# Lists of a mixture-of-experts kernel copied from a DRAM table instead of computed by matmuls, and a new order of row sums at its end

## The reference, cut to what matters

```
scores = sigmoid(t @ router_w)                    # 384 tokens x 64 experts
... group-limited choice: 8 experts for each token
w = take(scores, idx); w = w / sum(w) * 2.5       # gates of the chosen ones
hid = silu(t @ w_gate[e]) * (t @ w_up[e]) * gate  # FF = 256, per expert
routed = sum over e of hid @ w_down[e]
x = x + gate2 * (routed + shared expert)
y = rmsnorm(x, final_g)
```

## Time and profile before

| | us |
|---|---|
| median of 3 runs (lowest to highest) | 1182.12 (1181.52 to 1184.41) |
| the profiled execution | 1182.67 |
| its span, first to last instruction | 1180.8 |
| before the expert loop | 0 to about 516 |
| expert loop | about 516 to 1141 |
| end | about 1141 to 1180.8 |
| mean granted TensorE clock | 0.987 of full |

### The profile page before, as it was taken

One profiled execution on the slowest core, in us unless ns is written; L12 is line 12 of the kernel. 1 busy time (PEld: TensorE's weight loads), 2 busy tenths in 40 slices (PEclk: granted clock), 3 DMA queues, 4 the chain that ended last, 5 costly groups with the idle time before them and its releaser, 6 DMA issues.

```text
span 1180.8 us, 16797 instructions
## 1 busy us (share of the span) xinstructions
PE 1130.6 (96%) x5641; PEld 921.2 (78%) x5641; DVE 1029.9 (87%) x1378; ACT 801.3 (68%) x996; POOL 241.5 (20%) x184
## 2 busy tenths in 40 slices
PE   4999999998999999989999999999999999999995
PEld 1699999864557798658888888888888888888862
DVE  4769999989996565769999999999999999999976
ACT  6543232777873642648888888888888888888832
POOL 1000000001113001212523223333233323232210
PEclk9999999998999989999999999999999999999998
DMA  9673446635447227858999999999999999999994
GB/s 347 187 183 107 141 150 169 180 119 173 160 131 227 76 92 260 324 227 319 382 370 373 368 381 367 378 362 354 348 352 356 367 357 376 363 378 361 355 415 176
DMA packets 123036, 328.06 MB, mean 278 GB/s; under 512 B 28281, under 2 KB 69848, under 8 KB 98152
## 3 DMA queue, kind: packets, MB, share of 16 engines
q1 hardware_dynamic: 98368, 289.34, 66.7%
q0 software_dynamic: 21648, 33.80, 8.5%
q10 hardware_dynamic: 2968, 4.26, 1.0%
HBM read 326.66 MB, written 41.66 MB: 312 GB/s over the span
## 4 chain that ended last, share of the span: by engine, by line
PE 86%; DVE 5%; ACT 4%; DMA 3%; issue 1%; SPq 0%; POOLq 0%; ACTq 0%; DVEq 0%
PE bank L1755 22%; PE bank L1757 22%; PE bank L1756 22%; PE bank L1765 8%; PE bank L1950 2%; ACT hi L819 2%; PE bank L1938 2%; PE bank L2081 1%; DMA raw<-in_mod_w_dram 1%; DVE lo L1194 1%; PE bank L1771 1%; PE bank L1772 1%; PE bank L2200 1%; DMA xg<-h_d,ixt 1%; PE bank L2230 1%
## 5 line engine op out<-in xcount | busy, mean ns | idle before, releaser
L1463 DVE TENSOR_TENSOR lgu<-raw,hgu 128x2048 fp32r<-128x2048 f32 x128 | 292.1, 2282 | 2.3 <-ACT hgu L1072 2.3
L1072 ACT ACTIVATE hgu<-raw 128x2048 fp32r<-128x2048 f32 x128 | 245.2, 1916 | 0.0
L1755 PE MATMUL bank<-hgu,xgh 128*128 128x512 f32 x512 | 206.6, 404 | 0.4 <-issue 0.3
L1757 PE MATMUL bank<-hgu,xgl 128*128 128x512 f32 x512 | 201.4, 393 | 0.0
L1756 PE MATMUL bank<-lgu,xgh 128*128 128x512 f32 x512 | 199.7, 390 | 0.0
L1592 DVE TENSOR_TENSOR lo<-raw,hi 128x2048 fp32r<-128x2048 f32 x64 | 147.6, 2306 | 25.7 <-ACT hi L1081 21.5
L1194 DVE TENSOR_TENSOR lo<-raw,hi 128x2048 fp32r<-128x2048 f32 (+2 forms) x57 | 125.6, 2207 | 29.6 <-ACT hi L819 29.6
L777 POOL DMA_INDIRECT xg<-h_d,ixt x64 | 66.3, 1036 | 391.2 <-DVE gsl L1565 367.6
L786 POOL DMA_INDIRECT y_d<-ys,ixt x62 | 130.2, 2100 | 48.3 <-ACT ys L1114 28.6
L1292 DVE SCALAR_TENSOR_TENSOR zb<-zb,cwt 128x400 f32<-128x400 f32 x240 | 135.6, 630 | 0.6
L1081 ACT ACTIVATE hi<-raw 128x2048 fp32r<-128x2048 f32 x64 | 122.9, 1921 | 14.6 <-DMA raw<-in_exp_w_down_dram 14.4
(11 more groups left out here) (312 smaller groups left out, 2085.7 us busy)
## 6 DMA issues: line engine op xcount, KB each, us to landing
raw<-in_exp_w_gate_dram SPq DMA_DIRECT2D x64, 1024.0 KB
raw<-in_exp_w_up_dram SPq DMA_DIRECT2D x64, 1024.0 KB
raw<-in_exp_w_down_dram SPq DMA_DIRECT2D x64, 1024.0 KB
raw<-in_mod_w_dram SPq DMA_DIRECT2D x20, 1024.0 KB, 5.2
raw<-in_w_in_dram SPq DMA_DIRECT2D x16, 512.0 KB, 5.3
raw<-in_w_in_dram SPq DMA_DIRECT2D x8, 1024.0 KB, 5.3
mraw<-in_mod_w_dram SPq DMA_DIRECT2D x4, 1024.0 KB, 15.7
raw<-in_w_o_attn_dram SPq DMA_DIRECT2D x4, 1024.0 KB, 5.0
```

The source lines that it names most:

```text
L1072: act.activation(hgu[k % 2][:, :, w, :], src, ACT.Copy).then_inc(ghi_done, 1)
L1463: dve.tensor_tensor(lgu[k % 2][:, :, w, :], src, hgu[k % 2][:, :, w, :].bitcast(F32), ALU.subtract).then_inc(glo_done, 1)
L1755: pe.matmul(out, ah, bh, start=first, stop=False)
L1757: return pe.matmul(out, al, bh, start=False, stop=last)
```

## The change

1. Lists. Only the first 19 experts (`ON_TENSOR`) get their list by `onehot` and `token_list`. For these and the later ones, 24 small DMAs write a table `lists_d` in DRAM: one 16-byte entry (token row, destination row, gate) for each token and choice. `entry_rows` prepares the entries' rows on VectorE ahead of the loop, `entry_gates` their gates, two in each of steps 2 to 13, and `write_lists` issues two writes of 128 entries on GpSimd's queue in the same steps, behind that step's gather and scatter. In step 14 the table is read back to SBUF (`listed`). For experts from 19 on, `list_of` is two copies from `listed`.
2. The table is filled with ones near the start of the kernel by a DMA from GpSimd's queue.
3. A second block of 8 steps is written out ahead of the device loop (`BLOCKS`).
4. The load of `fgr` moves from ahead of the loop to the step with `left == 3`, the 62nd.
5. End: tile 0 takes residual and gate after row 5, then rows 6 and 7 scaled one by one; TensorE adds row 7 of tile 1 ahead of row 6 of tile 2.
6. Two pairs of semaphores are merged; two constants are added (88 columns).

```diff
+            pool.wait_ge(con_in, 16)
+            pool.dma_start(lists_d.rearrange(...), ones.unsqueeze(1).to_broadcast([P, NJ * 4 // P, P])).then_inc(lists_out, 16)
...
+            def write_lists(first):
+                for n in (first, first + 1):
+                    t, u = n // TOPK, n % TOPK
+                    pool.wait_ge(entry_done, n + 1)
+                    pool.indirect_dma_start(lists_d, bass.IndirectOffsetOnAxis(ap=entry_row[:, t, u:u + 1], axis=0),
+                                            entry[:, t, u, :], None,
+                                            bounds_check=P * NJ - 1, oob_is_err=False).then_inc(lists_out, 16)
...
+                if isinstance(j, int) and FIRST_SENT <= j < FIRST_SENT + 12:
+                    write_lists(2 * (j - FIRST_SENT))
+                if isinstance(j, int) and j == FIRST_SENT + 12:
+                    pool.wait_ge(lists_out, 16 * (NT * TOPK + 1))
+                    pool.dma_start(listed[:, :, :], lists_d.rearrange("(q j) v -> q j v", q=P)).then_inc(lists_out, 16)
...
+                if left == 3:
+                    listed_all = value(act, i * UNROLL + UNROLL)
+                    act.wait_ge(rtab_done, 1)
+                    act.wait_ge(list_done, listed_all)
+                    act.dma_start(fgr[:, :], final_g...partition_broadcast(P)).then_inc(tail_in, 16)
...
-            act.wait_ge(x1_out, 48)
-            act.dma_start(fgr[:, :], final_g...partition_broadcast(P)).then_inc(tail_in, 16)
...
+                if not isinstance(j, int) or j >= ON_TENSOR:
+                    dve.wait_ge(lists_out, 16 * (NT * TOPK + 2))
+                    dve.tensor_copy(ixt[:, k % UNROLL, :], listed[:, bass.ds(j, 1), 0:2]...bitcast(I32))
+                    dve.tensor_copy(gsl[:, k % UNROLL:k % UNROLL + 1], listed[:, bass.ds(j, 1), 2:3]...).then_inc(list_done, 1)
+                    return
...
+            def entry_rows():
+                dve.wait_ge(x1_out, 48)
+                (24 instructions on 128x192 and 128x24: keys, top 8 of them, row numbers by shifts and masks)
+            def entry_gates(first):
+                for n in (first, first + 1):
+                    ...
+                    dve.scalar_tensor_tensor(out=key_gate[:, n % 8, :], in0=keys[:, t, :], scalar=key8[:, t, u:u + 1],
+                                             in1=gates[:, t, :], op0=ALU.is_equal, op1=ALU.mult,
+                                             accum_out=entry[:, t, u, 2:3]).then_inc(entry_done, 1)
...
-                if left > 4:
+                if isinstance(j, int) and j + 4 < ON_TENSOR:
                     onehot(i, k + 4)
                 if left > 1:
                     turn_lo(i, k + 1)
+                if isinstance(j, int) and FIRST_SENT <= j < FIRST_SENT + 12:
+                    entry_gates(2 * (j - FIRST_SENT))
...
             shared_hidden(2)
+            entry_rows()
             in_order(dve, step)
...
-                if left > 3:
+                if isinstance(j, int) and j + 3 < ON_TENSOR:
                     token_list(i, k + 3)
...
             plus(5, 0)
-            plus(6, 0)
             based(0)
-            finished(0)
+            scaled_plus(6)
+            scaled_plus(7)
             finished(1)
...
-            for n in (5, 6, 7):
-                for t in (1, 2):
+            for n, t in ((5, 1), (5, 2), (6, 1), (7, 1), (6, 2), (7, 2)):
```

More of the change, by code:

```diff
@@ L50 @@
 NO_TOKEN = 4096
+KEY = 2048
+BLOCKS = 2
+ON_TENSOR = BLOCKS * UNROLL + 3
+FIRST_SENT = 2
 TAIL_SUMS = 4 * NT + 4
@@ L72, in constants @@
     parts["token"] = i[:, None] + P * np.arange(NT)[None, :]
+    parts["key"] = np.broadcast_to(KEY * (NE - np.arange(NE))[None, :], (P, NE))
+    parts["dest"] = (TOPK * parts["token"][:, :, None] + np.arange(TOPK)).reshape(P, NT * TOPK)
     at, n = {}, 0
@@ L277, in hybrid_step @@
         gsl = sb("gsl", [P, UNROLL], R + 8.375)
+        listed = sb("listed", [P, NJ, 4], A + 105)
+        entry = sb("entry", [P, NT, TOPK, 4], A + 7.25)
+        entry_row = sb("entry_row", [P, NT, TOPK], A + 7.625, I32)
+        keys = sb("keys", [P, NT, NE], A + 105)
+        gates = sb("gates", [P, NT, NE], A + 105.75)
+        key_gate = sb("key_gate", [P, 8, NE], A + 106.5)
+        key8 = sb("key8", [P, NT, TOPK], A + 108.5)
+        key_i, key_p, key_q, key_r = (sb(f"key_{n}", [P, NT, TOPK], R + 15.125 + 0.125 * i, I32)
+                                      for i, n in enumerate("ipqr"))
         sg = sb("sg", [P, FF], R + 9)
@@ L301, in hybrid_step @@
         y_d = dram("y_d", [T * TOPK, D])
+        lists_d = dram("lists_d", [P * NJ, 4])
         def conv_slot(k):
@@ L343, in hybrid_step @@
         cks_out = sem("cks_out")
[L344 to L345 removed]
+        zeros_done, sig_done, z_done, conv_step = (sem(n) for n in ("zeros_done", "sig_done", "z_done", "conv_step"))
+        sgs_out = [sem(f"sgs_out{i}") for i in range(2)]
         qtok_done, qrope_done, qT_act, qT_dve = (sem(n) for n in ("qtok_done", "qrope_done", "qT_act", "qT_dve"))
@@ L468, in in_order @@
             last = rounds_of(eng)
-            for k in range(UNROLL):
-                step(0, k)
-            with eng.Fori(1, last) as i:
+            for i in range(BLOCKS):
+                for k in range(UNROLL):
+                    step(i, k)
+            with eng.Fori(BLOCKS, last) as i:
                 for k in range(UNROLL):
@@ L1558, in list_of @@
                     p = got(dve, ("list", j))
-                else:
+                elif isinstance(j, int) and j < ON_TENSOR:
                     dve.wait_ge(list_filled, j - 1)
@@ L1693, in finished, with scaled_plus @@
             def finished(t):
[L1695 to L1704, removed]
-                        ins = dve.tensor_tensor(part[:, cols], psum[shared_banks[t][b]][:, :],
-                                                tg[:, cond_of(t), cols], ALU.mult)
-                    link(dve, "v", ins)
-                sums["all"] += 1
-                dve.tensor_tensor(acc[:, t, :], base, part, ALU.add).then_inc(sum_done, 1)
+                part = tout[:, t, :]
+                dve.wait_ge(g2_done, 2)
+                dve.wait_ge(sh_filled, t + 1)
+                for b in range(2):
+                    cols = slice(512 * b, 512 * b + 512)
+                    ins = dve.tensor_tensor(part[:, cols], psum[shared_banks[t][b]][:, :],
+                                            tg[:, cond_of(t), cols], ALU.mult)
+                link(dve, "v", ins)
+                sums["all"] += 1
+                dve.tensor_tensor(acc[:, t, :], tx[:, t, :], part, ALU.add).then_inc(sum_done, 1)
+            def scaled_plus(n):
+                late_landed(dve, n, 0)
+                part = row_tile(n, 0)
+                link(dve, "v", scaled(part, part, 0))
+                sums["all"] += 1
+                sums[0] = sums["all"]
+                dve.tensor_tensor(acc[:, 0, :], acc[:, 0, :], part, ALU.add).then_inc(sum_done, 1)
             def normed(t):
```

60 lines of the change are left out of this document (46 added, 14 removed).

## The result

The kernel before took 1181.82 us (median of 4 runs, 1180.68 to 1184.41), the changed kernel 1211.43 us (4 runs, 1210.40 to 1212.51). The ratio is 1.0246, with a 95% interval from 1.0228 to 1.0263, so about 29 us slower. The forecast was 1175.4 us, the range 1165 to 1188.

A forecast was written before the change was run, and what follows sets the result against it. The prediction took TensorE as the bound, with DMA and VectorE close behind. Its terms, -10 -1.7 -1 +2.5 +0.5 +1 +0.5 +0.5, were summed to -6.7 us, for a median of 1175.4 us, range 1165 to 1188.

The forecast's parts named there:

- the list term: Loop steps 16 to 60 without list matmuls on TensorE: 10 us less, ends 3 and 14.4 us.
- eleven waits in a row at 375: ScalarE waiting for down's weights, 645.54 to 742.17 us, at 375 GB/s: read as DMA engines just keeping up.
- DMA binds: Rival in the loop: DMA keeps steps at about 9.6 us, median about 1180.5 us, no change; chance 0.2.
- Everything follows: Rival in the loop: DMA keeps 9.35 us throughout and the writes hide, -15.6 us, 1166.5 us; chance 0.16.
- GpSimd's queue binds: Rival in steps 2 to 13: four queue instructions exceed the step, gathers fall behind, about 1195 us (milder 1187); chance 0.18.
- The tail: At the end, TensorE's swapped row sums let VectorE start tile 1 earlier: gain 1.7 us, at least 1.2.
- writes +2.5: Steps 2 to 13: table writes cost 2.5 us through late gathers and small DMA packets, ends 0 and 20.6.
- gates +0.5: VectorE's two `entry_gates` per step: 0.5 us charged once, for the first steps without lead, ends 0 and 2.
- read-back +1: Step 14: reading the table back arrives late for VectorE, 1 us lost, ends 0 and 3.
- `fgr` -1 and +0.5: Moved load: 1 us gained beside the early gather (0 to 1.8), 0.5 us lost in step 61 (0 to 1.4).
- 9.35 us after the lists: Sign of being right: TensorE's transposes 9.35 us apart after step 19, 9.667 before.
- ScalarE waiting for the weights of down in every later step: Sign of being wrong: ScalarE held up by DMA of down's weights in the later loop steps.

The follow-up runs named there:

- the kernel before with `slot` spread: Kernel before with one constant changed, position p of a list on partition 4*(p mod 32) + p/32: 1183.8 us, ratio 0.9994.
- The two kernels that differ by the copies: Changed kernel, position p on partition 4*(p mod 32) + p/32: all lists by matmul, table unused, 1184.4 us; with copies from the table, 1167.6 us.
- the changed kernel with the arrangement of before: Changed kernel with only the table's row formula inverted, position p on partition (p % 16) * 8 + p // 16 like the matmul lists: 1180.9 us, ratio 0.9982.
- the spread kernel: Changed kernel with position p on partition 4*(p mod 32) + p/32, in `slot` and the table's row formula: 1167.6 us, ratio 0.9871.
- The kernel with an unused table and its rows spread: Changed kernel, position p on partition 4*(p mod 32) + p/32, table written and read, all 64 lists by matmul, no copies: 1184.4 us, ratio 1.0018.

## Why the prediction was wrong, and where it was right

**The step that failed** is the one that carried the list term: "I take 10 us, near the first end because its stretch carries the same mix of loads, gathers and scatters". The bytes are the same. Their division over the engines isn't, since the lists from expert 19 on fill other partitions, and where the term said 10 us less the loop took 18.3 us more. The prediction treated DMA as one pool with a limit in GB/s, 375 or 415, and asked only how many bytes a step moves; with such a pool no arrangement can matter. The runs in which only the arrangement was changed showed 30 us for it in either kernel. The formula is in the change, and `slot`, which it was to match, in both kernels; that the places of the rows change could be read there, and it belonged among the rivals with a price for uneven engines. None of the rows that the prediction read shows the load of one engine, but the packet records of the same trace hold it, as the gather of expert 5 above shows.

**The sentence that should have warned** is the one about "eleven waits in a row at 375". The prediction read them as a limit of the whole group. In the kernel before with `slot` spread these waits are gone, at 379 and 369 GB/s in the same stretches, so they came from the eight engines that carried the rows.

**The list term** was right in its cause and, once the rows are spread, its upper end was nearer than the value taken: 14.4 us was the end, and from the seventh transposes to the last the trace has 536.34 us in place of 550.44, 14.1 less. The two kernels that differ by the copies are 16.8 us apart by their medians and 18.2 by their profiles: 14.1 there, 1.5 in the first steps, where the one with all matmuls had a stretch of low clock (below), and 1.3 each ahead of them and at the end. With the table in the arrangement of before, the loop from the seventh transposes to the last takes 542.74 us, 7.7 less than in the kernel before, in one profile; the difference of times is 4.4.

**The rivals.** *DMA binds* named about 1180.5 us; the changed kernel with the arrangement of before took 1180.9. With its eight busy engines DMA does bind there at times, at 0.96 and 369 GB/s and with steps up to 10.5 us. But the steps didn't stay at about 9.6 us, as this rival had it: most were 9.35 us. So its figure is in part luck, and it held for a kernel that was never the one predicted. *Everything follows*, 1166.5 us, is what the spread kernel does: 1167.6. The limit from the Trainium skill (DMA: Bandwidth & Descriptors, Specifications), about 358 GB/s, didn't hold: the spread kernel moved 374 GB/s for 360 us. *GpSimd's queue binds* came to the point it named, four instructions without a gap, and cost TensorE nothing: a write took 1.87 to 2.62 us, not 4.8, and the gathers are issued early enough.

**The tail**: 1.7 us forecast, 1.9 by the times (0.5 to 3.4), 1.7 by the trace.

**The small terms** (writes +2.5, gates +0.5, read-back +1, `fgr` -1 and +0.5, fill +0.5) make +4.0 us. The kernel with an unused table and its rows spread is 1.0018 x 1183.4 - 1183.4 = 2.1 us slower than the kernel before although it has the tail's 1.9 us: also 4.0, but each of the two is uncertain by over 1 us, and in the arrangement of before the same sum is 1.3 + 1.9 = 3.2. The sum agrees, its parts don't. `fgr` gained nothing, for the reason given above; the prediction asked what the load delayed, not what was next in line. The table's read-back was issued at 662.23 us in the changed kernel and nobody waited for it. The small packets were overpriced: the prediction had 8 packets of 16 bytes for each engine and write, 30 ns each, and the records show 16 packets of 128 bytes in all for one write, 15 ns each. In the first steps the seventh begins 51.0 us after the first, against 49.0 without a table, but 1.6 us of that are the low clock told of below; the spread kernel that uses its table has 49.4. Where the rest of the 4 us lies these runs don't show.

**The sum itself** is off by one: its terms add up to -7.7 us, not -6.7, so the forecast by its own terms was 1174.4 us. That doesn't bear on the failure.

**The signs that the prediction named**: 9.35 us after the lists, seen for four steps and then throughout the spread kernel; "ScalarE waiting for the weights of down in every later step", given as a sign of its being wrong, was the one that came.

## What to carry to other kernels

Rows of an indirect DMA are moved by the engine of their SBUF partition, so choose the partitions of a partly filled list as carefully as its length: fill one partition of each engine's eight before the second. When an engine waits for DMA while the DMA share is *below* its best, ask which engine is late before asking for fewer bytes. And a change that is meant to produce the same data another way should be held against the old in its order too, not only in its set.

## What the runs showed of the hardware

**Partition and engine.** The rows of gathers and scatters follow engine = 8*(q/64) + (q mod 32)/4, by the packets of a gather (46 rows) and a scatter (37 rows) followed engine by engine, and by the times (1181.5 to 1214.7 us for one constant). The Trainium skill (DMA: Bandwidth & Descriptors, The descriptor swizzle) has this formula; the trace agrees with it.

**The limit of one core alone** is higher than the 375 and 388 GB/s that looked like one: 396 GB/s for 40 us in the spread kernel, and 404 from 1100 to 1140 us:

```profile
1100.00:1140.00 40.00, 39.66 (x150) 26.59 (x149) 32.54 (x31) 18.80 (x26) 8.06 (x7) 1.00 1.01 404
```

The Trainium skill (Perfetto Trace Analysis, Roofline) says that 358 GB/s is a core's share when both of a pair are at work, and that one alone may reach about 435; this trace agrees so far as it goes.

**A short wait and TensorE's clock.** Two kernels that differ by the copies of step 16 and later had the same wait at the same place, behind the fifth transposes. In the first (unused table) the granted clock fell, in the second (with copies) it didn't:

```profile
547.80 0.77 PE L1838 MATMUL bank<-hgu,xgh 128*128 128x512 f32 x1 [1.86 <-DVE lgu L1503]
```

```profile
540.00:550.00 10.00, 8.14 (x38) 6.72 (x37) 10.00 (x15) 8.68 (x10) 5.35 (x3) 0.89 0.80 270
550.00:560.00 10.00, 10.00 (x49) 8.40 (x48) 10.00 (x15) 4.92 (x8) 7.52 (x4) 0.94 0.96 375
```

```profile
546.58 0.47 PE L1843 MATMUL bank<-hgu,xgh 128*128 128x512 f32 x1 [1.85 <-DVE lgu L1502]
```

```profile
540.00:550.00 10.00, 8.14 (x43) 6.79 (x42) 10.00 (x16) 8.26 (x9) 5.36 (x3) 1.00 0.78 288
```

The columns are those of the other stretches. The matmul behind the wait took 0.77 us in place of 0.47, and the step 13.32 us in place of 11.72: 0.89 and 0.94 over 20 us is some 3.4 us at 1.2 GHz among 2.4, which costs half of that. The changed kernel had it too (0.91 from 540 to 560 us). What decides it these runs don't show; 1.6 us of a difference between two profiles can be this alone.
